# One half unit of weights moved between two visits of the RWKV group loop

## The chip, the cores and the metric

The kernel runs on one core of one Trainium2 chip. The metric is the device time in microseconds (us). Before the change three runs took 3044.5, 3040.24 and 3040.24 us, so the median is 3040.24 us.

## The reference

A trunk of two layers on 256 tokens of width 2048. Layer 0 is a mixer whose first half is stick-breaking attention (8 heads of 128) and whose second half is an RWKV-7 group (16 heads of 64), layer 1 a gated delta rule; each is followed by a residual and norm and by a squared-ReLU MLP of width 8192. Everything is float32. The part that matters here is the RWKV group and the attention beside it:

```
z = q @ k.T * d**-0.5;  log_keep = where(mask, log_sigmoid(-z), 0)
a = exp(where(mask, z + reverse_cumsum(log_keep), -inf));  o_sb = a @ v
w_log = -softplus(-(w0 + tanh(w_lo) @ w_up)) - 0.5;  decay = exp(-exp(w_log))
a = sigmoid(a0 + a_lo @ a_up);  g = sigmoid(g_lo) @ g_up
kk = l2_normalize(k * k_k);  k = k * (1 + (a - 1) * k_a)
S = S * w_t - (S kk_t) (kk_t a_t)^T + v_t k_t^T;  y_t = S r_t      # per token, per head
y = (y - mean(y)) * rsqrt(var(y) + eps) * lnx_g + lnx_b            # per head
o_rw = (y + sum(r * k * r_k) * v) * g
h = concat(o_sb, o_rw) @ w_out
```

The kernel computes the recurrence in four chunks of 64 tokens: inside a chunk a triangular inverse by doubling (five levels), between chunks a state handed on.

## The kernel before, in words

**Weights.** Every matrix product takes its weights from HBM in units of 256 input rows (two halves of 128) by 384 or 512 columns; a panel has 8 units. The product is done as three: `wh x ah`, `wh x al`, `wl x ah`. So each unit goes through three engines before TensorE can use it. SP loads it into `raw` (8 buffers), ScalarE casts it to `wh` (L887), VectorE subtracts to get the low half `wl` (L1357); `wh` and `wl` have 4 buffers each. TensorE then does the unit in two halves of 9 matmuls of 256 columns (narrow, mode B) or 6 of 512 (wide, mode A), all recorded at L421. Semaphores: `landed`, `hi_ready`, `lo_ready` forward, `unit_used` back.

**Groups and visits.** Layer 0's input projection is one panel for the low-rank parts and eight groups of two narrow panels (16 units, 32 halves). While group i is projected, the mixer of group i-1 (`mix0`) is computed. The mixer is a generator on each of TensorE, ScalarE and VectorE with the same 28 stops, here called visits 0 to 27. At each visit an engine does its part of the mixer and then the weights that the table `HOPS0` gives to that visit. The order is thus written out by hand and each engine's queue is strictly in this order. `hop_of(half, halves, hops)` turns the table, read as shares, into the visit of each half. On TensorE `drive` does the halves of a visit one by one. On ScalarE and VectorE `interleave` does the cast or subtraction of unit u+2 (`LEAD` = 2) at the visit where TensorE does the first half of unit u, that is half 2u. With `wait` = 1 the projection's results are copied out of the accumulator one visit after the last half of a panel.

`HOPS0` is used by six rounds of a loop and by one written out after it (mixers 0 to 6). `HOPS0Z` is the same table with a last share of 4; with it the eighth mixer is interleaved with 28 wide units of the output projection, 56 halves over 35 shares.

**The visits that matter**, on TensorE (with the lines that feed them):

- 1: low-rank products (L498 to L501), the values turned and the scores (L504 to L507).
- 2: the norm of the keys, L512. 3: the running sum of the logs, L517 and L518.
- 4: the attention product, L521 and L522; it waits for the exp of ScalarE, L980, which waits for VectorE's L1535. In between, ScalarE makes gates and powers (L949 to L977; L971 reads L512's result), VectorE the scan and the operands (L1510 to L1539; L1535 reads L518's result).
- 5: the Gram products, L534. 6: the turned operands, L550; ScalarE copies them (L989, L991).
- 7 to 17: five doublings of the inverse. At an odd visit X is turned and multiplied (L557, L565), VectorE masks the product (L1565); at an even visit the update (L581), VectorE adds it (L1572). From the third doubling on VectorE also does a piece of the next group's token shift at each visit.
- 18: L604 and L610. 19 to 25: the four chunks. L634 gives what is added to the state, VectorE scales it (L1597 for chunk 0, L1599 for the others) and adds the old state (L1602); the next chunk's L622 or L625 reads the new state; L638 and L639 give the chunk's output. Chunk n's first matmul (L622, L625) is at visits 20, 22, 24, its output at 19, 21, 23, 25.
- 26: the norm's mean, L644, after ScalarE has copied the four outputs (L1026). 27: the variance, L648.

The PSUM banks, the semaphores and the arithmetic of all these are not touched by the change.

Of the kernel before, what the change touches and what calls it, by code (L numbers as in the profile page):

```python
# [56 lines left out]
B_MLP1 = B_OUT1B + 8  # L57


HOPS0 = (3, 3, 2, 2, 2) + 16 * (1,) + (0, 1, 0, 1, 0, 1, 1)  # L60
HOPS0Z = HOPS0[:-1] + (4,)
HOPS_LORA = 16 * (1,)
HOPS1S = (3, 3, 3, 3, 3, 2, 3) + 14 * (1,) + (3, 2, 3, 3, 3)
# [56 lines left out]
def interleave(mixer, hops, units, one, ends, hook, ahead, begun=False, late=None, u0=0,  # L120
               wait=None):

    if not begun:
        for u in range(LEAD):
            one(u0 + u)
    wait = wait or (1 if mixer else 2)
    hops = hops if mixer else units * (1,)
    for y in range(len(hops) + wait + 1):  # L130
        if mixer and y < len(hops):
            next(mixer)
        for u in range(units):
            if hop_of(2 * u, 2 * units, hops) == y and (ahead or u + LEAD < units):
                one(u0 + u + LEAD)
        for j, e in enumerate(ends):
            after = y - hop_of(2 * e + 1, 2 * units, hops) - wait
            if after in (0, 1):
                hook(j, after)
    if mixer:  # L140
        assert next(mixer, "over") == "over"
    if late:
        late()
# [20 lines left out]
def trunk(nc, stop, x, w384, w512, wba, consts, c0, c1, prm0, lora, conv, rows1, normw, ln, out):  # L164
    ctx = ExitStack()
    with ctx:
# [209 lines left out]
        def _(pe):  # L376
# [58 lines left out]
            def drive(one, units, u0=0, mixer=None, hops=()):  # L435

                if mixer is None:
                    for u in range(units):
                        one(u0 + u)
                    return  # L440
                for y in range(len(hops)):
                    next(mixer)
                    for h in range(2 * units):
                        if hop_of(h, 2 * units, hops) == y:
                            one(u0 + h // 2, h % 2)
                assert next(mixer, "over") == "over"
# [204 lines left out]
            def group0(i):  # L651
                return blocks(i * 2 + P_GROUPS0, i * 2 + P_GROUPS0, "B", A, (0, 1), NARROW)
# [4 lines left out]
            with pe.Fori(1, GROUPS - 1) as i:  # L657
                drive(group0(i), 2 * UNITS, 0, mix0(i - 1), HOPS0)
            drive(group0(GROUPS - 1), 2 * UNITS, 0, mix0(GROUPS - 2), HOPS0)

# [217 lines left out]
        def _(act):  # L878
# [164 lines left out]
            def group0(i, first=False, last=False):  # L1043
                n = i * 2 + P_GROUPS0

                def one(u):
                    if last and u >= 2 * UNITS:
                        split(P_OUT0, u - 2 * UNITS, WIDE)
                    else:
                        split(n + u // UNITS, u % UNITS, NARROW)  # L1050

                def hook(j, after):
                    if after:
                        return
                    used(n, j * UNITS + UNITS - 1)
                    if j == 0:
                        if not first:

                            act.wait_ge(S("shifted"), i * 2 - 1)
                        nc.scalar.copy(pb[:, :, 1:T + 1], r2(pp[0][:, 0:3 * T], a=3)).then_inc(S("evacuated"), 1)  # L1060
                    else:
                        if not first:

                            act.wait_ge(S("scores"), i)
                        st(go(sbq[:, 0, :], pp[1][:, 0:T], ACT.Copy, scale=SB_SCALE))
                        nc.scalar.copy(sbq[:, 1:3, :], r2(pp[1][:, T:3 * T], a=2)).then_inc(S("evacuated"), 1)
                return 2 * UNITS, one, (7, 15), hook, True, True

            def wide(n):
                return lambda u: split(n + u // UNITS, u % UNITS, WIDE)  # L1070
# [7 lines left out]
            with act.Fori(1, GROUPS - 1) as i:  # L1078
                st.enter(i - 1, PER)
                interleave(mix0(i - 1), HOPS0, *group0(i))  # L1080
            st.leave(GROUPS - 2)
            interleave(mix0(GROUPS - 2), HOPS0, *group0(GROUPS - 1, last=True))
            interleave(mix0(GROUPS - 1), HOPS0Z, 28, wide(P_OUT0), (), nothing, True, begun=True)
# [259 lines left out]
        def _(dve):  # L1343
# [281 lines left out]
            def narrow(n, last=False):  # L1625
                def one(u):
                    if last and u >= 2 * UNITS:
                        split(P_OUT0, u - 2 * UNITS, WIDE)
                    else:
                        split(n + u // UNITS, u % UNITS, NARROW)  # L1630
                return one
# [15 lines left out]
            with dve.Fori(1, GROUPS - 1) as i:  # L1647
                st.enter(i - 1, PER)
                interleave(mix0(i - 1), HOPS0, 2 * UNITS, narrow(i * 2 + P_GROUPS0), (), nothing, True, True)
            st.leave(GROUPS - 2)  # L1650
# [429 lines left out]
```

## Time and profile before

| | |
|---|---|
| median of 3 runs | 3040.24 us |
| profiled execution | 3040.92 us |
| its span | 3039.3 us |
| TensorE busy | 2956.7 us |
| VectorE busy | 1797.6 us |
| ScalarE busy | 1452.7 us |
| read from HBM | 486.76 MB |

The profile is of one execution. Busy times overlap, so they don't add up to the span. A matmul's start is recorded and its end is modelled, so consecutive matmuls overlap in the timeline, and "idle before" is measured from a modelled end. Times in the timeline count from the span's start. The first mixer round begins at about 71 us, the eighth ends at about 580 us.

### The profile page before, as it was taken

The page shows a single profiled execution, that of the slowest core. Times are in us where ns is not written, and L with a number is a line of the kernel's source. Part 1 is how long each engine was busy: PE and PEld are TensorE (multiplying, and loading weights), DVE is VectorE, ACT ScalarE, POOL GpSimd, SP SyncE. Part 2 cuts the span into 40 slices and gives each one's busy share as a digit, 9 for nine tenths or more (in the row PEclk, how much of TensorE's full clock was granted, in tenths as well). Part 3 has the DMA queues.
Part 4 walks back from the last instruction along what each step waited for, and adds up shares of the span by engine and source line. Part 5 has one row for each costly group of instructions (what it writes and reads, how often), then busy time and mean ns, then how long its engine had stood idle before and what let it go on. Part 6 is the DMA issues. An engine that isn't in the chain of part 4 may idle for free.

```text
span 3039.3 us, 55921 instructions
## 1 busy us (share of the span) xinstructions
PE 2956.7 (97%) x22084; PEld 2603.5 (86%) x22084; DVE 1797.6 (59%) x2375; ACT 1452.7 (48%) x2241; POOL 13.1 (0%) x28
## 2 busy tenths in 40 slices
PE   8999999899999999999999999999999999999997
PEld 8888887688888888889999997999977888888886
DVE  4655565665554555564667665566667545555565
ACT  4544544344443434435566664556654434444442
POOL 0000000000000000000000000000000000000000
PEclk9999999999999999999999999999999999999998
DMA  7333334455555555544333433544335555555553
GB/s 231 109 111 106 107 118 139 166 202 193 189 189 191 186 194 188 192 160 139 120 139 133 139 133 136 177 141 137 133 122 219 189 192 187 194 191 191 193 188 111
DMA packets 156999, 491.86 MB, mean 162 GB/s; under 512 B 15584, under 2 KB 50528, under 8 KB 155776
## 3 DMA queue, kind: packets, MB, share of 16 engines
q1 hardware_dynamic: 154032, 476.18, 45.9%
q0 software_dynamic: 2224, 11.69, 1.0%
q8 instruction: 160, 2.62, 0.3%
q10 hardware_dynamic: 544, 1.05, 0.1%
q14 instruction: 39, 0.32, 0.0%
HBM read 486.76 MB, written 2.10 MB: 161 GB/s over the span
## 4 chain that ended last, share of the span: by engine, by line
PE 91%; DVE 5%; ACT 2%; issue 1%; DMA 0%; ACTq 0%; SPq 0%; DVEq 0%
PE pp L421 45%; PE mp L421 11%; PE pp L405 8%; PE mp L405 8%; PE pp L407 4%; PE mp L407 4%; PE mp L820 1%; PE mp L784 1%; PE mp L768 1%; PE mp L760 1%; DVE wl L1357 1%; ACT wh L887 1%; PE mp L826 1%; PE mp L565 0%; PE mp L581 0%
## 5 line engine op out<-in xcount | busy, mean ns | idle before, releaser
L1357 DVE TENSOR_TENSOR wl<-raw,wh 128x1024 fp32r<-128x1024 f32 (+1 forms) x936 | 1101.2, 1184 | 842.5 <-ACT wh L887 839.5
L887 ACT CAST wh<-raw 128x1024 fp32r<-128x1024 f32 (+1 forms) x936 | 944.1, 1018 | 856.4 <-PE pp L421 284.9
L421 PE MATMUL pp<-aT,wh 128*128 128x256 f32 x4704 | 897.6, 291 | 4.8 <-DVE wl L1357 4.8
L421 PEld LDWEIGHTS pp<-aT,wh 128*128 128x128 f32 x4704 | 733.0, 191 | 20.4 <-issue 5.5
L421 PE MATMUL pp<-aT,wl 128*128 128x256 f32 x2352 | 665.7, 283 | 0.0
L421 PEld LDWEIGHTS pp<-aT,wl 128*128 128x128 f32 x2352 | 450.0, 191 | 0.0
L405 PE MATMUL pp<-aT,wh 128*128 128x512 f32 x1024 | 364.0, 400 | 0.1
L421 PE MATMUL pp<-wh,hTh 128*128 128x512 f32 x896 | 358.6, 400 | 4.0 <-DVE wl L1357 2.6
L405 PE MATMUL mp<-aT,wh 128*128 128x512 f32 x1024 | 360.0, 396 | 0.0
L421 PE MATMUL pp<-wh,hTl 128*128 128x512 f32 x896 | 349.7, 390 | 0.0
L421 PE MATMUL pp<-wl,hTh 128*128 128x512 f32 x896 | 349.2, 390 | 0.0
L407 PE MATMUL pp<-aT,wl 128*128 128x256 f32 x1024 | 287.9, 281 | 0.0
L407 PE MATMUL mp<-aT,wl 128*128 128x256 f32 x1024 | 286.5, 280 | 0.0
L405 PEld LDWEIGHTS pp<-aT,wh 128*128 128x128 f32 x1024 | 194.0, 189 | 47.4 <-issue 0.7
L405 PEld LDWEIGHTS mp<-aT,wh 128*128 128x128 f32 x1024 | 192.2, 188 | 46.3
L421 PEld LDWEIGHTS pp<-wh,hTh 128*128 128x128 f32 x896 | 168.2, 188 | 42.1 <-DVE wl L1357 2.9
L421 PE MATMUL mp<-wh,hTl 128*128 128x512 f32 x512 | 199.2, 389 | 0.0
L421 PE MATMUL mp<-wh,hTh 128*128 128x512 f32 x512 | 199.2, 389 | 0.0
L421 PE MATMUL mp<-wl,hTh 128*128 128x512 f32 x512 | 199.2, 389 | 0.0
L421 PEld LDWEIGHTS pp<-wh,hTl 128*128 128x128 f32 x896 | 168.2, 188 | 35.9
L421 PEld LDWEIGHTS pp<-wl,hTh 128*128 128x128 f32 x896 | 168.4, 188 | 32.9 <-issue 0.5
L407 PEld LDWEIGHTS pp<-aT,wl 128*128 128x128 f32 x1024 | 194.8, 190 | 0.1
(301 smaller groups left out, 2673.5 us busy)
## 6 DMA issues: line engine op xcount, KB each, us to landing
raw<-in_w_dram SPq DMA_DIRECT2D x800, 512.0 KB, 3.3
raw<-in_w_dram SPq DMA_DIRECT2D x136, 384.0 KB, 3.5
ws<-in_ln_dram POOLq DMA_DIRECT2D x8, 1024.0 KB, 7.5
out_dram<-xres SPq DMA_DIRECT2D x8, 256.0 KB, 2.1
ws<-in_lora_dram POOLq DMA_DIRECT2D x8, 192.0 KB, 3.5
xres<-in_x_dram ACTq DMA_DIRECT2D x2, 512.0 KB, 6.4
xres<-in_x_dram SPq DMA_DIRECT2D x2, 512.0 KB, 7.2
ws<-in_c_dram POOLq DMA_DIRECT2D x1, 576.0 KB, 7.0
```

Source lines behind the costliest of these rows:

```text
L405: mm(o, wh[:, slot, kk, c], aT[:, k, :, :].rearrange("p a b -> p (a b)"), start=first is not None and kk == 0, stop=False, skip_group_chec ...
L407: last = mm(o[:, 0:T], wl[:, slot, kk, c], ah[:, k, :], start=False, stop=end and kk == 1, skip_group_check=True)
L421: last = mm(o, lhs, rhs, start=opens and m == 0, stop=end and kk == 1 and m == 2, skip_group_check=True)
L760: last = nc.tensor.transpose(mb[2][:, h * P:(h + 1) * P], Xc[:, 2 * h:2 * h + 2, :].rearrange("p c t -> p (c t)"), ident)
L768: last = mm(mb[hf][half(c), h * P:h * P + 32], At[half(hf), c, h, half(hf)], Xp[:, :, 0, :], start=h == 0, stop=True, skip_group_check=True)
L784: last = mm(mb[2 + c][half(hf), h * P:h * P + 32], XTc[half(c), h, hf, :], Yn1[half(c), 4 * hf + h, :], start=h == 0, stop=True, skip_grou ...
L820: last = mm(bank[:, h * P:(h + 1) * P], lhs[:, h, :], rhs[:, h, :], start=h == 0, stop=True, skip_group_check=True)
L826: last = mm(bank[:, j * T:(j + 1) * T], lhs[:, j, :], rhs[:, 2 * j:2 * j + 2, :], start=j == 0, stop=True, skip_group_check=True)
L887: nc.scalar.copy(wh[:, q % RING, :, 0:width], raw[:, q, :, 0:width]).then_inc(S("hi_ready"), 1)
L1357: tt(wl[:, q % RING, :, 0:width], raw[:, q, :, 0:width], f(wh[:, q % RING, :, 0:width]), ALU.subtract).then_inc(S("lo_ready"), 1)
```

## The change

One share is taken from visit 1 and one is given to visit 25. `HOPS0Z` is built from `HOPS0` and changes with it.

```diff
-HOPS0 = (3, 3, 2, 2, 2) + 16 * (1,) + (0, 1, 0, 1, 0, 1, 1)
+HOPS0 = (3, 2, 2, 2, 2) + 16 * (1,) + (0, 1, 0, 1, 1, 1, 1)
 HOPS0Z = HOPS0[:-1] + (4,)
```

Worked out with `hop_of`, the halves of a round of 32 fall like this (number of the half at each visit):

```
visit   0      1      2    3    4      5   6  ... 20  21  22  23  24  25  26  27
before  0 1 2  3 4 5  6 7  8 9  10 11  12  13 ... 27  -   28  -   29  -   30  31
after   0 1 2  3 4    5 6  7 8  9 10   11  12 ... 26  -   27  -   28  29  30  31
```

The casts and subtractions (even halves) are at visits 0, 0, 1, 2, 3, 4 both times, and then at 5, 7, 9, 11, 13, 15, 17, 19, 22, 26 before and at 6, 8, 10, 12, 14, 16, 18, 20, 24, 26 after. The copy out of the first panel (ScalarE, L1060) goes from visit 9 to visit 10.

## Rows read from the trace of the kernel before

**Rows 1.** The page, busy time of TensorE: us, share, instructions.

```profile
...
PE 2956.7 (97%) x22084; PEld 2603.5 (86%) x22084; DVE 1797.6 (59%) x2375; ACT 1452.7 (48%) x2241; POOL 13.1 (0%) x28
...
```

**Rows 2.** Waits of TensorE, 0 to 700 us: total, times, longest, all us.

```profile
...
PE mp L521 <- ACT ws L980: 8.1, 7, 1.2
...
PE mp L644 <- ACT ws L1026: 6.9, 8, 0.9
PE mp L471 <- DVE xres L1441: 6.9, 4, 5.3
PE pp L421 <- DVE wl L1357: 5.1, 11, 1.4
PE mp L625 <- DVE ws L1602: 3.9, 7, 0.9
...
```

**Rows 3.** Timeline of TensorE, attention product: start, length, instruction, idle before.

```profile
...
74.32 0.48 PE L421 MATMUL pp<-aT,wh 128*128 128x256 f32 x2
...
77.63 0.59 PE L512 MATMUL mp<-ws 128*128 128x256 f32 x2
...
80.86 0.39 PE L518 MATMUL mp<-ws,cc 128*128 128x128 f32 x2
81.00 0.48 PE L421 MATMUL pp<-aT,wh 128*128 128x256 f32 x2
...
84.55 0.70 PE L521 MATMUL mp<-ws 128*128 128x256 f32 x2 [1.16 <-ACT ws L980]
85.09 0.39 PE L522 MATMUL mp<-ws 128*128 128x128 f32 x2
85.72 0.50 PE L421 MATMUL pp<-aT,wh 128*128 128x256 f32 x2 [0.25 <-DVE wl L1357]
...
```

**Rows 4.** Timeline of TensorE, last chunk to the norm's mean.

```profile
...
121.21 0.50 PE L421 MATMUL pp<-aT,wh 128*128 128x256 f32 x2
...
122.39 0.55 PE L638 MATMUL mp<-ws 128*128 128x64 f32 x4
122.78 0.44 PE L639 MATMUL mp<-ws 128*128 128x128 f32 x2
124.07 0.70 PE L644 MATMUL mp<-ws 128*128 128x256 f32 x2 [0.85 <-ACT ws L1026]
...
```

**Rows 5.** Timeline of ScalarE, the exp before the attention product.

```profile
...
83.97 0.53 ACT L980 ACTIVATE ws<-ws 128x384 f32<-128x384 f32 x1 [0.90 <-DVE ws L1535]
...
```

**Rows 6.** Waits of ScalarE and VectorE for TensorE, 60 to 600 us.

```profile
...
ACT ws L971 <- PE mp L512: 0.4, 1, 0.4
...
DVE ws L1535 <- PE mp L518: 2.3, 1, 2.3
...
```

**Rows 7.** Timelines of ScalarE, VectorE and TensorE, first doubling.

```profile
...
92.51 0.37 ACT L991 COPY ws<-mp 128x256 f32<-128x256 f32 x1
...
93.80 0.84 ACT L887 CAST wh<-raw 128x768 fp32r<-128x768 f32 x1
...
94.67 0.96 DVE L1357 TENSOR_TENSOR wl<-raw,wh 128x768 fp32r<-128x768 f32 x1 [1.19 <-ACT wh L887]
95.54 0.28 DVE L1572 TENSOR_TENSOR ws<-ws,mp 128x128 f32<-128x128 f32 x1
...
94.48 0.43 PE L581 MATMUL mp<-ws 64*64 64x32 f32 x16
...
```

**Rows 8.** Timelines of VectorE and TensorE, third and last chunk.

```profile
...
119.03 0.96 DVE L1357 TENSOR_TENSOR wl<-raw,wh 128x768 fp32r<-128x768 f32 x1 [0.32 <-ACT wh L887]
120.03 0.35 DVE L1599 SCALAR_TENSOR_TENSOR ws<-mp,ws 128x128 f32<-128x128 f32 x1
...
119.30 0.38 PE L634 MATMUL mp<-ws 128*128 128x128 f32 x2
...
```

**Rows 9.** Windows: length, busy per engine, granted clock, DMA share, GB/s.

```profile
...
84.00:124.00 40.00, 37.73 (x492) 34.04 (x492) 23.14 (x49) 16.44 (x32) 0.00 (x0) 1.00 0.38 120
...
606.00:612.00 6.00, 4.11 (x16) 2.91 (x17) 5.89 (x10) 1.75 (x3) 0.00 (x0) 0.50 0.00 0
...
```

## The prediction

> **What bounds the kernel now.** I read the page first: TensorE is busy for 97% of the span [rows 1], so a change can pay only where TensorE waits, and costs what it makes TensorE wait. Next the waits of TensorE over the first 700 us, where the RWKV visits lie [rows 2]. The reader is to see that they are few: 8.1 us before the attention product (L521), 6.9 us before the norm's mean (L644), 5.1 us for low halves of weights (L421), 3.9 us for the last chunk's state (L625). Then the timeline of TensorE over one loop round. It repeats: L521 starts at 84.55 us [rows 3] and every 59.53 us after that, with the same waits to 0.01 us, so one round can be worked out. There are eight mixer rounds: six in the loop, a seventh written out with the same table, an eighth in which the output projection fills the visits (56 halves by 35 shares).
>
> The printed idle time is taken against a modelled matmul end, so I count from start to start. From L518 (80.86) to the next matmul without a wait are 0.14 us; so L522 (85.09) would be followed at 85.23, but the next half starts at 85.72 [rows 3]: 0.49 us lost where 0.25 are printed. From L639 (122.78, so the next could start at about 122.93) to L644 (124.07) are 1.14 us, where 0.85 are printed [rows 4].
>
> One half unit is 9 matmuls. Alone between two steps it takes 1.18 us (121.21 to 122.39) [rows 4]; three in a row take 3.31 us (74.32 to 77.63) [rows 3], so one more or less in a run is (3.31 - 1.18) / 2 = 1.07, with the 9 matmuls at 0.12 us 1.08 us.
>
> **The change, part by part.** Nothing is added or taken away on any queue: the same 32 halves, casts, subtractions and DMAs. Old half 5 leaves visit 1; from there each half is done one place later (visits 2 to 24 hold the half before the one they held), and visit 25 gets half 29. The cast on ScalarE and the subtraction on VectorE hang on the even halves, so between visits 5 and 20 they change from odd visits to even ones, and one goes from visit 22 to 24. SP's next load of a unit follows its subtraction by up to two visits; no engine waits for a landing in these rounds, so 0.
>
> *Visits 1 to 3, ahead of the attention product.* TensorE comes 1.08 us earlier to L512, L517 and L521. What L521 waits for is the exp L980 (83.97), which waits for a subtraction of VectorE, L1535 [rows 5]. Does this chain wait for TensorE anywhere between the scores and L521? In the eight rounds ScalarE waited for the key norm (L971) once, 0.4 us, and VectorE for the running sum (L1535) once, 2.3 us [rows 6], both in the eighth. In the other seven the chain is bound by its own engines, and the casts and subtractions of visits 0 to 4 are the same in number and place. So L521 stays at 84.55 and the wait before it grows by the whole 1.08 us, from 1.16 to about 2.24 printed: 0. If the chain did follow TensorE it would be a gain of 1.08; that end is a rival.
>
> *Visit 4.* Before, the first half there is the first of unit 5, whose low part comes late (0.25 printed, 0.49 from start to start) [rows 3]. After, the second half of unit 4 stands there, whose weights lie ready, and unit 5 comes 1.08 us later. The loss goes: -0.49 a round. Next late would be the operands of L534; on VectorE they stand ahead of the very subtraction that ended at 85.7, so they are there.
>
> *Visit 6 and the first doubling (a new wait).* VectorE now has a subtraction at visit 6, ahead of the masked product L1565 of visit 7. It needs the cast, which ScalarE can begin only behind the copy L991 (92.51, 0.37 long): about 92.78 to 93.62 with the 0.84 of the cast at 93.80. The subtraction runs until about 94.61, L1565 starts near 94.52 (0.87 behind it, as 94.67 to 95.54) and ends near 94.81; L581, now at 94.48 [rows 7], would start near 94.87. That is +0.39 a round. From below 0 (the cast gets ahead of the copy), from above a whole subtraction, 0.96; I take the worked one. At the other doublings the subtraction stands behind the state sum (0.28) and a shift piece (0.48), 1.8 us ahead of the next masked product: 0.28 + 0.48 + 0.96 fit, no wait.
>
> *Visits 18 to 24.* Before, the subtraction of visit 22 (119.03, 0.96 long) holds back L1599, which starts at 120.03 although L634 (119.30, 0.38 long) was done at 119.7 [rows 8]. It moves to visit 24, where VectorE idles: -0.24 at L625. The new ones at visits 18 and 20 come ahead of L1597 and L1599. By the same hand count L1597 comes 0.45 us later against a reserve of 0.7 at the next L622, and L1599 0.07 later, without reserve. Net -0.17. The floor here is -0.50 (all of L625's printed wait), the ceiling +0.96 (a subtraction wholly in the way).
>
> *Visit 25.* Half 29 takes 1.15 to 1.2 us where 1.14 are lost; what L644 waits for is ready 1.27 us after L639's start, and 0.15 + 1.15 of these are now used. The wait disappears and L644 keeps its distance to L639 within 0.05: 0. The end of the round (halves 30 and 31, the next round's visit 0, the norm's chain to the next scores) hangs on L644 and moves with it.
>
> Sum of a steady round: 0 - 0.49 + 0.39 - 0.17 + 0 = -0.27 us; seven rounds -1.9. The cover that visit 1 gave up is paid in full (1.08), and that won at visit 25 is worth as much (1.14 less the half itself): they cancel, and what is left are side effects.
>
> *Round seven* has at visit 22 a wide subtraction (1.2 us), so a wait of 0.9 at L625 (the longest) [rows 2] shrinks by 0.4 more. *Round eight:* visits 1 to 4 hold 3, 4, 3, 3 halves in place of 5, 3, 3, 4. Its wait is one of 1.4 us at L421 (the longest) [rows 2], before the first half of unit 7, behind VectorE's 2.3 us for L518 [rows 6]. After, L518 comes one half of this kind (1.37 us, 6 matmuls of 0.23) earlier and the wait moves to unit 6, 2.9 us long; L521 stays with one half less done, 1.38, of which visit 25 gives back 1.14: +0.25. All rounds: -1.9 - 0.4 + 0.25 = about -2.05 us.
>
> The profiled execution took 3040.92 us around a span of 3039.3; the sum puts it at 3038.9. The median of the runs shown is 3040.24, 0.68 lower, so the forecast is 3038.2 us.
>
> By printed idle times the sum would be 1.08 - 0.85 - 0.25 + 0.39 - 0.17 = +0.2 a round, +1.4 in all. The Trainium skill, Perfetto Trace Analysis (Tensor Engine Instruction), has a matmul's reported end as an estimate; the 0.25 us by which the row at 80.86 outlasts the next start agrees, so I stay with starts.
>
> **The rivals.**
> - *The chain to L521 follows TensorE.* For it: one wait each at L971 and L1535; against it: both in round eight. It gives 1.08 more in each of seven rounds: 3038.2 - 7.6 = 3030.6 us.
> - *No new wait at the first doubling*: 0.39 x 7 less, 3035.5 us. For it there is only that the order isn't seen in any row of before.
> - *The subtractions on even visits cost more.* A late L1597 (visit 19) crosses the 0.25 us left before L622, or L581 starts slowly after its wait. From there each round loses what is over; at 0.6 (two thirds of a subtraction) the time is 3038.2 + 4.2 = 3042.4 us, slower than before, though within the bound.
> - *The clock falls.* TensorE idles 2.24 us at L521 instead of 1.16. In 84 to 124, which holds the waits of a whole round, it was granted 1.00 (2.4 GHz); after the idle of 5.3 us before L471 [rows 2] it was granted 0.50 (1.2 GHz) in 606 to 612, with 4.11 us busy [rows 9]. Some 6 us busy at half speed until it rose again are 3 us lost; seven times 21: 3059 us, slower by over the bound. It decides where a wait of 2.24 us is enough to bring the clock down; the waits at full clock in [rows 2] reach to 1.4 us. The Trainium skill, TensorE: Matmul & The Clock Gate (What's actually happening), has the throttled state as the default that activity lifts; the row at 0.50 agrees in kind.
>
> **How the numbers follow.** Forecast 0.72; no new wait 0.11; dearer even visits 0.09; chain follows TensorE 0.05; clock 0.03. A measurement of this kernel can tell about 0.2% (6.1 us) from no change; the first three cases lie within it but for 0.01 of the second and 0.01 of the third. Faster: 0.05 + 0.01 = 0.06; slower: 0.03 + 0.01 = 0.04; same 0.90. Range: from below the second case to above the third, 3033 to 3043 us; outside are the fourth and fifth and the tails. The runs of before were 3040.24 twice and 3044.5, so they scatter more than the change weighs.
>
> **What the profile after would show.** L521's wait near 2.24 us in the first seven rounds; none at L644, and none at L421 right behind L522; a new one of about 0.3 us at L581 of the first doubling; L625's down from 0.50 to about 0.25; a round of 59.26 us in place of 59.53; in round eight 2.9 us before a half of L421. I would be wrong if L521's wait didn't grow (the chain moved), if L644's stayed, or if a granted clock under 1.00 stood between 60 and 490 us.

## The result, and the profile after

The changed kernel takes 3049.22 us (median of 8 runs, 3048.27 to 3052.18) where the kernel before took 3040.89 beside it (8 runs, 3038.35 to 3044.5). The ratio is 1.0029 with a 95% interval of 1.0021 to 1.0038: 8.3 us slower by the medians. The forecast was 3038.2 us and a range up to 3043. The profiled execution took 3052.18 us, its span is 3050.5.

The page, busy time of TensorE, against [rows 1]:

```profile
...
PE 2967.1 (97%) x22084; PEld 2613.9 (86%) x22084; DVE 1796.1 (59%) x2375; ACT 1455.0 (48%) x2241; POOL 13.1 (0%) x28
...
```

TensorE does the same 22084 matmuls but is busy 10 us longer. Matmuls that take longer mean a lower clock, not a wait. Next the waits of TensorE over the first 700 us, against [rows 2] (total, times, longest, in us):

```profile
...
PE mp L521 <- ACT ws L980: 13.2, 7, 1.9
...
PE pp L421 <- DVE wl L1357: 4.7, 4, 2.7
PE mp L581 <- DVE ws L1565: 2.8, 7, 0.4
PE mp L622 <- DVE ws L1602: 2.4, 7, 0.4
PE mp L625 <- DVE ws L1602: 1.7, 7, 0.6
...
```

L644 is gone, L521 went from 8.1 to 13.2 us, L581 came in with 0.4 us a round, L625 fell to 0.2 in the loop, L622 rose. All of this was forecast in kind, and the forecast's sum of it is a gain of 2; it doesn't explain a loss of 8 us. So I looked at the granted clock. These are windows of 6 us from each L521 on, one for each of the seven rounds, and then one from the wait of 2.7 us for a low half (L421) in round eight (length, busy time of each engine, granted clock, DMA share, GB/s), against [rows 9]:

```profile
...
84.00:90.00 6.00, 5.28 (x50) 5.04 (x54) 3.88 (x8) 2.35 (x4) 0.00 (x0) 0.72 0.42 132
145.00:151.00 6.00, 5.57 (x80) 5.19 (x80) 4.97 (x10) 2.20 (x4) 0.00 (x0) 1.00 0.46 146
204.00:210.00 6.00, 5.34 (x51) 5.15 (x55) 3.91 (x8) 2.35 (x4) 0.00 (x0) 0.72 0.42 132
265.00:271.00 6.00, 5.61 (x70) 5.33 (x70) 3.55 (x7) 2.16 (x4) 0.00 (x0) 0.72 0.47 147
326.00:332.00 6.00, 5.90 (x82) 5.52 (x83) 4.96 (x10) 1.87 (x4) 0.00 (x0) 1.00 0.47 146
385.00:391.00 6.00, 5.68 (x70) 5.49 (x70) 3.48 (x7) 2.09 (x4) 0.00 (x0) 0.72 0.48 159
446.00:452.00 6.00, 5.94 (x71) 5.59 (x72) 3.51 (x7) 1.83 (x4) 0.00 (x0) 0.72 0.50 158
514.00:520.00 6.00, 5.33 (x16) 4.28 (x17) 3.93 (x4) 0.97 (x2) 0.00 (x0) 0.72 0.59 195
...
```

The clock was granted in full behind L521 in rounds two and five only. In rounds one, three, four, six and seven, and in round eight behind its own wait, the mean is 0.72: read in steps of 1 us, 1.00 (2.4 GHz) at first, then 0.50 (1.2 GHz) for some 3 us. Such a stretch is called a fall below. In the same windows of the kernel before every round reads 1.00. In all 8 runs of the changed kernel the mean clock is 0.988 or 0.989, in the profiled run of before 0.992.

What a fall costs is read by comparing rounds. TensorE in round two, which has none, against [rows 3] and [rows 4]; first from L512 to L534:

```profile
...
137.31 0.28 PE L421 MATMUL pp<-aT,wl 128*128 128x256 f32 x1
137.69 0.70 PE L512 MATMUL mp<-ws 128*128 128x256 f32 x2
...
145.43 0.70 PE L521 MATMUL mp<-ws 128*128 128x256 f32 x2 [1.88 <-ACT ws L980]
...
146.11 0.48 PE L421 MATMUL pp<-aT,wh 128*128 128x256 f32 x2
146.43 0.28 PE L421 MATMUL pp<-aT,wl 128*128 128x256 f32 x1
...
148.43 0.78 PE L534 MATMUL mp<-ws 64*64 64x128 f32 x20
...
```

And in round one, which has one:

```profile
...
84.72 0.70 PE L521 MATMUL mp<-ws 128*128 128x256 f32 x2 [1.89 <-ACT ws L980]
85.26 0.39 PE L522 MATMUL mp<-ws 128*128 128x128 f32 x2
85.40 0.52 PE L421 MATMUL pp<-aT,wh 128*128 128x256 f32 x2
85.72 0.41 PE L421 MATMUL pp<-aT,wl 128*128 128x256 f32 x1
85.94 0.63 PE L421 MATMUL pp<-aT,wh 128*128 128x256 f32 x2
86.36 0.41 PE L421 MATMUL pp<-aT,wl 128*128 128x256 f32 x1
...
89.23 1.10 PE L534 MATMUL mp<-ws 64*64 64x128 f32 x32
...
```

The two halves of visit 4 take 2.32 us in round two (146.11 to 148.43) and 3.83 us in round one (85.40 to 89.23); a group of three matmuls there takes 0.64 us (85.94 to 86.58) where it takes 0.36. From L521 to the next L521 are 59.23 us behind rounds two and five (145.43 to 204.66) and 60.71 to 60.74 behind rounds one, three, four and six. So a fall costs 1.5 us. Without one the round is 0.30 us shorter than the 59.53 of before: the forecast was 0.27.

The books of the two profiled executions: from L521 of round one to that of round seven +4.15 us, which is four falls of 1.49 less six times 0.30; from there to L644 of round eight +3.04 us (136.14 for 133.10), which holds the falls of rounds seven and eight. Together +7.2 us, in a difference of medians of 8.3. The profiled span is longer by a further 4 us, behind the RWKV rounds; single runs of either kernel differ by as much, so they aren't taken apart here. But one more fall lies there, in layer 1, behind a wait that the change doesn't touch. It is the wait for a low half of weights; first the changed kernel, then the kernel before, each with the window of 6 us behind it:

```profile
...
1429.81 0.51 PE L421 MATMUL pp<-aT,wh 128*128 128x256 f32 x2 [1.75 <-DVE wl L1357]
...
1430.00:1436.00 6.00, 6.00 (x39) 6.00 (x39) 6.00 (x12) 5.55 (x10) 0.00 (x0) 0.72 0.54 182
...
```

```profile
...
1423.28 0.50 PE L421 MATMUL pp<-aT,wh 128*128 128x256 f32 x2 [1.76 <-DVE wl L1357]
...
1423.00:1429.00 6.00, 5.52 (x44) 5.32 (x45) 6.00 (x12) 5.26 (x9) 0.00 (x0) 1.00 0.48 161
...
```

The same wait of 1.76 us is followed by a fall in one kernel and by none in the other.

### The profile page after: what moved, and what is told of

The parts are those of the page before. It is cut to its first block, busy times and chain, and to the rows that moved or that the text cites. A ratio compares the mean times of both kernels' runs of the same rounds, so it can differ in the third digit from the quotient of the medians.

```text
span 3050.5 us, 55919 instructions
## 1 busy us (share of the span) xinstructions
PE 2967.1 (97%) x22084; PEld 2613.9 (86%) x22084; DVE 1796.1 (59%) x2375; ACT 1455.0 (48%) x2241; POOL 13.1 (0%) x28
## 4 chain that ended last, share of the span: by engine, by line
PE 91%; DVE 5%; ACT 3%; issue 2%; DMA 0%; ACTq 0%; SPq 0%; DVEq 0%
PE pp L421 45%; PE mp L421 11%; PE pp L405 8%; PE mp L405 8%; PE pp L407 4%; PE mp L407 4%; PE mp L820 1%; ACT wh L887 1%; PE mp L784 1%; PE mp L768 1%; PE mp L760 1%; DVE wl L1357 1%; PE mp L826 1%; PE mp L581 0%; DVE xres L1437 0%
## 5 line engine op out<-in xcount | busy, mean ns | idle before, releaser
L421 PE MATMUL pp<-aT,wh 128*128 128x256 f32 x4704 | 906.9, 293 | 2.8 <-DVE wl L1357 2.8
L421 PEld LDWEIGHTS pp<-aT,wh 128*128 128x128 f32 x4704 | 740.5, 193 | 16.9 <-issue 5.5
L421 PE MATMUL pp<-aT,wl 128*128 128x256 f32 x2352 | 670.1, 285 | 0.0
L421 PEld LDWEIGHTS pp<-aT,wl 128*128 128x128 f32 x2352 | 454.5, 193 | 0.0
L421 PE MATMUL pp<-wh,hTh 128*128 128x512 f32 x896 | 359.1, 401 | 5.4 <-DVE wl L1357 4.0
L421 PE MATMUL pp<-wh,hTl 128*128 128x512 f32 x896 | 350.4, 391 | 0.0
L421 PE MATMUL pp<-wl,hTh 128*128 128x512 f32 x896 | 349.7, 390 | 0.0
L421 PEld LDWEIGHTS pp<-wh,hTh 128*128 128x128 f32 x896 | 168.7, 188 | 43.5 <-issue 3.6
L421 PEld LDWEIGHTS pp<-wh,hTl 128*128 128x128 f32 x896 | 168.5, 188 | 36.0
L421 PE MATMUL mp<-wh,hTh 128*128 128x512 f32 x512 | 199.2, 389 | 0.0
L421 PE MATMUL mp<-wl,hTh 128*128 128x512 f32 x512 | 199.2, 389 | 0.0
L421 PE MATMUL mp<-wh,hTl 128*128 128x512 f32 x512 | 199.2, 389 | 0.0
L421 PEld LDWEIGHTS pp<-wl,hTh 128*128 128x128 f32 x896 | 168.8, 188 | 33.0 <-issue 0.5
```

Of the source, the lines that this page charges most:

```text
L421: last = mm(o, lhs, rhs, start=opens and m == 0, stop=end and kk == 1 and m == 2, skip_group_check=True)
```

## The experiments

Theory A: the wait before L521, 1.16 us before and 1.9 after, is now long enough that TensorE's clock falls. Theory B: the slowdown comes from what moved on the other engines (subtractions at even visits) or from the half at visit 25. Falls in the table are counted over the seven rounds of one profiled execution, by the granted clock behind L521. Those in round eight and in layer 1 come on top and are gathered behind experiment 10. Ratios are to the kernel before on the same chip.

| kernel | wait at L521, us | falls | round without, with a fall, us | ratio, 95% interval |
|---|---|---|---|---|
| before | 1.16 | 0 | 59.53 | |
| changed | 1.89 | 5 | 59.23, 60.72 | 1.0029 (1.0021 to 1.0038) |
| 1: visit 1 to 4 | 1.9 | 6 | 60.07, 61.57 | 1.0057 (1.0043 to 1.0071) |
| 2: visit 4 to 25 | 1.16 | 0 | 58.67 | 0.9972 (0.9963 to 0.9981) |
| 3: changed, filled | 0.59 | 0 | 59.21 | 1.0005 (0.9996 to 1.0014) |
| 4: changed, filled less | 1.45 | 0 | 59.21 | 0.9997 (0.9988 to 1.0006) |
| 5: two from visit 1 | 1.15 and 1.17 | 0 | 60.08 | 1.0005 (0.9995 to 1.0014) |
| 6: visit 20 to 25 | 1.16 | 0 | 58.79 | 0.9982 (0.9973 to 0.9991) |
| 7: changed, two tables | 1.89 | 4 | 59.0, 60.5 | 1.0000 (0.9991 to 1.0009) |
| 8: as 2, two tables | 1.16 | 0 | 58.44 | 0.9970 (0.9958 to 0.9982) |
| 9: changed, filled least | 1.71 | 1 | 59.23, 60.71 | 1.0003 (0.9993 to 1.0014) |
| 10: changed, late exp | 2.97 | 7 | -, 61.8 (63.1 in round one) | 1.0059 (1.0042 to 1.0075) |

**1. The longer wait alone.**

```diff
-HOPS0 = (3, 3, 2, 2, 2) + 16 * (1,) + (0, 1, 0, 1, 0, 1, 1)
+HOPS0 = (3, 2, 2, 2, 3) + 16 * (1,) + (0, 1, 0, 1, 0, 1, 1)
```

> Built from the kernel before; one half goes from visit 1 to visit 4, nothing else moves: visit 25 stays empty, the casts and subtractions from visit 5 on stay at the odd visits. Theory A (the longer wait before L521 lets TensorE's clock fall to 1.2 GHz): the wait printed is 1.9 us as in the changed kernel, the granted clock falls to 0.50 behind it in most of the seven rounds, and a round is 59.53 + 1.08 - 0.49 = 60.1 us without a fall and 61.6 with one; with five falls and one in round eight the time is 3040.9 + 4.1 + 9 = about 3054 us. Theory B (the slowdown comes from the subtractions at even visits and from the half at visit 25): neither is here, no fall matters, 3040.9 + 4.1 = about 3045 us.

3057.65 us against 3041.65. Behind L521 of rounds one, two and seven:

```profile
...
82.00:88.00 6.00, 5.33 (x79) 5.10 (x79) 3.89 (x9) 3.08 (x5) 0.00 (x0) 1.00 0.44 132
142.00:148.00 6.00, 5.26 (x30) 5.21 (x31) 3.90 (x8) 3.18 (x5) 0.00 (x0) 0.72 0.40 126
...
450.00:456.00 6.00, 5.45 (x31) 5.40 (x31) 3.79 (x7) 3.15 (x5) 0.00 (x0) 0.72 0.46 140
...
```

Rounds two to seven fall, round one doesn't. The tail and the even visits are as before, and yet the falls are there: A. The falls are six, as many as expected, but all in the seven rounds and none in round eight. The time is 3.7 us above the expected; one more fall in layer 1 is part of it, the rest stays open.

**2. The same tail, the half from visit 4.**

```diff
-HOPS0 = (3, 3, 2, 2, 2) + 16 * (1,) + (0, 1, 0, 1, 0, 1, 1)
+HOPS0 = (3, 3, 2, 2, 1) + 16 * (1,) + (0, 1, 0, 1, 1, 1, 1)
```

> Built from the kernel before; the half for visit 25 is taken from visit 4, behind the attention product, instead of visit 1; from visit 5 on the order is that of the changed kernel. Theory A (clock): the wait before L521 stays at 1.16 us, no fall; a round is 59.53 - 1.08 (visit 4) + 0.39 (L581) - 0.15 (L622 and L625) = 58.7 us, so seven rounds give -6 us: about 3035 us. Theory B (even visits and visit 25): it is as slow as the changed kernel, 3046 to 3049 us.

3031.93 us against 3041.65: faster than both kernels. Its waits of TensorE over 700 us show the old L521 and the new L581 side by side, and L644 doesn't appear:

```profile
...
PE mp L521 <- ACT ws L980: 8.2, 7, 1.2
...
PE mp L581 <- DVE ws L1565: 2.8, 7, 0.4
...
```

From visit 5 on this kernel is the changed one, so B is refuted. The time is 3 us below the expected: round eight was left out of that sum, and it is 1.5 us shorter (70.71 us from round seven's L521 to its own, before 72.19).

**3 and 4. The wait filled with useless work.** Both are built on the changed kernel; the edit of 3, and in 4 a single matmul of 256 columns:

```diff
+                for _ in range(2):
+                    mm(mb[3][:, 0:384], tri, sbb, start=True, stop=True, skip_group_check=True)
                 pe.wait_ge(S("attn"), m1)
```

> Built from the changed kernel; two matmuls of 384 columns (1.3 us together) whose result is overwritten stand at visit 4 ahead of the wait for the exp. They do no useful work; they only keep TensorE busy in the time in which it would wait. Theory A (clock): the wait printed falls from 1.9 to about 0.6 us, L521 doesn't start later, no clock falls, every round is 59.23 us: 3040.9 - 2.1 = about 3039 us, that is 1.5 us less for each fall avoided. Theory B (order of the other engines): useless work can't help, 3049 us.

> As the kernel with two filling matmuls, but one of 256 columns (about 0.4 us): the wait printed is about 1.5 us, between the 1.16 of before and the 1.9 of the changed kernel. Theory A: fewer falls than the five of the changed kernel, each still worth 1.5 us; 3039 to 3046 us. Theory B: 3049 us. If the falls are as many as with 1.9 us, the length of the wait between 1.5 and 1.9 doesn't decide.

3043.03 and 3041.61 us against 3041.65. The timeline of TensorE in 3, round two (the fill moved the lines: L523 is the attention product), and the windows of 4 behind the attention product of rounds one and seven:

```profile
...
143.22 0.70 PE L523 MATMUL mp<-ws 128*128 128x256 f32 x2 [0.59 <-ACT ws L982]
...
```

```profile
...
82.00:88.00 6.00, 5.36 (x79) 5.11 (x79) 4.97 (x10) 2.35 (x4) 0.00 (x0) 1.00 0.41 132
...
437.00:443.00 6.00, 5.07 (x76) 4.82 (x77) 4.98 (x10) 2.35 (x4) 0.00 (x0) 1.00 0.38 118
...
```

No round of either falls. Adding some 10 or 3 us of useless matmuls takes away 7 to 9 us against the changed kernel, each taken against the kernel before beside it: the strongest sign for A, for nothing else was moved. In round eight, where the fill doesn't stand before the wait of 2.7 us, 3 still has a fall and 4 has none. There the attention product doesn't wait either, so the fill of 3 costs its own 1.3 us (512.25 to 513.54); with the fall it is the larger part of the 4 us by which 3 stays above its expected 3039.

**5. Two halves taken from visit 1** (on the changed kernel).

```diff
-HOPS0 = (3, 2, 2, 2, 2) + 16 * (1,) + (0, 1, 0, 1, 1, 1, 1)
+HOPS0 = (3, 1, 2, 2, 3) + 16 * (1,) + (0, 1, 0, 1, 1, 1, 1)
```

> Built from the changed kernel; one more half goes from visit 1 to visit 4, so that two fewer stand ahead of L521 than before. Theory A (how long TensorE idles before L521, with where in time it falls, decides whether the clock falls): part of the added idleness shows at L512, the rest at L521, at least 2.2 us in all there; the clock falls in all seven rounds instead of five or six, each costing 1.5 us, and a fall-free round would be 59.23 + 0.6 to 1.08 = about 60 us: 3041 + 7 x 0.7 + 7 x 1.5 + 2 = about 3058 us. Rival (a fall happens with a fixed share of rounds whatever the wait): again five or six of seven, about 3056 us; the granted clock of each round tells them apart, not the time.

3042.67 us against 3040.99, and no fall: a miss. It wasn't a longer wait, as I had meant it, but two short ones:

```profile
...
PE mp L512 <- ACT ws L955: 8.2, 7, 1.2
PE mp L521 <- ACT ws L980: 8.1, 7, 1.2
...
```

TensorE idles more than in the changed kernel (2.3 us a round in these two places), but in pieces of 1.2 us with 6 us of matmuls between them, and the clock stays. Half 4 went to visit 2, and with it one of the two casts that ScalarE did between L955 and L980 went behind L980. So L521 comes 7.01 us behind L512 (76.62 to 83.63), not 7.74; that is why the second wait didn't grow.

**6. The half from visit 20** (on the kernel before).

```diff
-HOPS0 = (3, 3, 2, 2, 2) + 16 * (1,) + (0, 1, 0, 1, 0, 1, 1)
+HOPS0 = (3, 3, 2, 2, 2) + 15 * (1,) + (0,) + (0, 1, 0, 1, 1, 1, 1)
```

> Built from the kernel before; the half for visit 25 is taken from visit 20, between two state chunks; through visit 19 nothing changes, so casts and subtractions stay at odd visits. Theory A: L521's wait stays 1.16 us, no fall; L644's wait goes (-1.14 + half), at visit 20 TensorE waits about 0.5 us for U instead of doing the half of 1.15: a round is 0.5 to 0.8 us shorter, 3041.6 - 4 to 5.5 = about 3037 us. Theory B (a half at visit 25 itself does harm): no faster than before, 3042 us or more.

3034.91 us against 3040.99, rounds of 58.79 us. A half moved from visit 20 to visit 25 is a gain; one at visit 25 does no harm.

**7 and 8. Two tables.** TensorE's `drive` gets a table of its own, ScalarE and VectorE keep `HOPS0`. In 7 it is the changed table, in 8 that of 2:

```diff
+HOPS0P = (3, 3, 2, 2, 1) + 16 * (1,) + (0, 1, 0, 1, 1, 1, 1)
-                drive(group0(i), 2 * UNITS, 0, mix0(i - 1), HOPS0)
+                drive(group0(i), 2 * UNITS, 0, mix0(i - 1), HOPS0P)
```

> TensorE follows the changed table, ScalarE and VectorE keep the table of before: TensorE's halves move as in the changed kernel, the casts and subtractions don't. Theory A (clock): the wait before L521 is still 1.9 us and the clock still falls in five or six of seven rounds; only the 0.39 us at L581 and the 0.35 at L622 change: 3049 - 2 = about 3047 us. Theory B (the subtractions at even visits): the slowdown is gone, 3039 us or less.

> The half for visit 25 from visit 4 on TensorE alone; ScalarE and VectorE keep the table of before. Against the kernel with the half from visit 4 on all engines (round 58.67 us, 0.39 of it the wait at L581): the L581 wait goes, the waits at L622 and L625 are 0.19 and 0.50 as before instead of 0.35 and 0.19: a round of about 58.4 us, no fall: 3031.9 - 2 = about 3030 us. Rival (the wait moves on to the next product of the doubling): 3032 us, the same.

7 takes 3041.09 us against 3040.99: 6 us less than expected, though the falls haven't gone. Behind the attention product of rounds one and two:

```profile
...
84.00:90.00 6.00, 5.59 (x66) 5.39 (x70) 3.61 (x7) 3.02 (x5) 0.00 (x0) 0.72 0.46 134
144.00:150.00 6.00, 5.06 (x76) 4.81 (x77) 4.98 (x10) 3.08 (x5) 0.00 (x0) 1.00 0.36 116
...
```

Rounds one, three, five and six fall (60.5 us), two, four and seven don't (59.0); round eight has none, for its wait of 2.7 us has gone too, and from L523 of round seven to that of round eight are 68.90 us where the kernel before has 72.19. So the useful part of the change and four falls cancel here. By time alone this would have spoken for B; the clock of each round speaks for A. That a round with the same wait of 1.9 falls or not, and that round eight stopped waiting so long, I hadn't counted on. 8 takes 3032.45 us against 3040.99; the L581 wait is gone and the rounds are 58.44 us, 0.23 less than in 2. The medians don't resolve this: by time alone it could as well be the rival, "3032 us, the same"; it is the length of the rounds that speaks against it.

**9. A still shorter fill** (one matmul of 64 columns) and **10. A later exp** (both on the changed kernel). The edit of 10 (`PER` is the number of ScalarE's counted steps in a round; the two copies add two):

```diff
                 act.wait_ge(S("loga"), m1)
+                for _ in range(2):
+                    st(nc.scalar.copy(sba, sba))
+                    st.settle()
                 go(sba, sba, ACT.Exp).then_inc(S("attn"), 1)
-            PER = 16
+            PER = 18
```

> As the kernel with one filling matmul, but of 64 columns: the wait printed before L521 is about 1.7 us, between the 1.45 us at which no clock fell in seven rounds and the 1.9 at which it fell in four to six. Theory (the length of one unbroken wait decides, with its place in time): some rounds fall, fewer than with 1.9, zero to four; time 3041 to 3047 us.

> Built from the changed kernel; ScalarE copies a tile onto itself twice between its wait for VectorE and the exp L980, which makes L521 later by 0.9 to 1.1 us in one unbroken wait of 2.8 to 3.0 us. The copies change no value. Theory (the length of one unbroken wait decides): the clock falls in all seven rounds, where the wait of 1.9 gave five; a round without a fall would be 59.23 + 1.0, with it 61.7 us; 3039 + 7 + 10.5 + 2 = about 3058 us. Rival (a fixed share of the rounds falls, whatever the wait over 1.5 us): five or fewer falls again, about 3055 us; the granted clock of each round tells it.

9: 3042.61 us against 3041.43; a wait of 1.71 us and one fall, in round one, with round two after it free:

```profile
...
84.00:90.00 6.00, 5.32 (x50) 5.13 (x54) 3.94 (x8) 2.35 (x4) 0.00 (x0) 0.72 0.40 128
145.00:151.00 6.00, 5.60 (x80) 5.21 (x81) 4.97 (x10) 2.18 (x4) 0.00 (x0) 1.00 0.48 147
...
```

10: 3058.98 us against 3041.43; a wait of 2.97 us and a fall in every round, in rounds one and seven one of double length:

```profile
...
85.00:91.00 6.00, 5.77 (x30) 5.37 (x34) 2.61 (x4) 2.01 (x4) 0.00 (x0) 0.50 0.50 140
148.00:154.00 6.00, 5.71 (x70) 5.38 (x70) 2.67 (x5) 2.07 (x4) 0.00 (x0) 0.72 0.50 145
210.00:216.00 6.00, 5.94 (x71) 5.68 (x72) 2.62 (x5) 1.83 (x4) 0.00 (x0) 0.72 0.57 157
271.00:277.00 6.00, 5.13 (x42) 4.88 (x46) 3.25 (x5) 2.61 (x5) 0.00 (x0) 0.72 0.45 133
333.00:339.00 6.00, 5.29 (x47) 4.98 (x50) 3.09 (x4) 2.45 (x5) 0.00 (x0) 0.72 0.46 130
395.00:401.00 6.00, 5.41 (x62) 5.10 (x66) 2.97 (x4) 2.35 (x4) 0.00 (x0) 0.72 0.44 132
457.00:463.00 6.00, 5.71 (x30) 5.31 (x34) 2.66 (x4) 2.06 (x4) 0.00 (x0) 0.50 0.51 143
...
```

Over the kernels the falls rise with the one unbroken wait: none of seven at 0.59, 1.16 and 1.45 us, one at 1.71, four to six at 1.9, seven at 2.97. One fixed share for all waits over 1.5 us doesn't fit one of seven at 1.71 beside seven of seven at 2.97. Each count is that of one profiled execution.

The falls outside the seven rounds say the same, and something more. Behind the wait of 2.74 us in round eight the clock fell in four kernels (changed, 3, 9, 10) and didn't in two (1, 4). Behind the wait of 1.75 or 1.76 us in layer 1, which stands in all twelve kernels and which no edit touches, it fell in seven (changed, 1, 2, 4, 5, 7, 9) and didn't in five (before, 3, 6, 8, 10). So the length of the wait makes a fall more likely and doesn't decide it alone.

## Why the prediction was wrong

*The step that failed* is the choice between the forecast and the fourth rival, "the clock falls". In the forecast's sum the clock is put at nothing; the runs show six falls, 9 us, in its place. The rival named the place (L521), the cause (a wait grown by what visit 1 gave up) and the sign; I gave it 0.03, because the waits of before at full clock reached 1.4 us in [rows 2] and the one behind which it had fallen was 5.3, and took the gap between as if it were on my side. Nothing in the rows said so, and the trace of before holds a narrower gap that I didn't read. At 1423.28 it has the wait of 1.76 us at full clock. And the wait of 5.3 us at L471 begins at about 601.0 and ends at 606.29, while the clock falls well inside it:

```profile
...
603.00:604.00 1.00, 0.00 (x0) 0.00 (x0) 1.00 (x2) 0.00 (x0) 0.00 (x0) 0.94 0.00 0
604.00:605.00 1.00, 0.00 (x0) 0.00 (x0) 0.86 (x4) 0.47 (x3) 0.00 (x0) 0.50 0.00 0
...
```

So some 2.8 us of idling had been enough there. The forecast wait of 2.24 us lay between these two, where the trace was silent; that bound should have been in the range.

*Its price was mis-sized*: 3 us for each of seven falls. A fall behind L521 measures 1.5 us, since the half clock lasts some 3 us there and not the 8 from L471's start on (606.29 to about 614.1), and there are five of seven and one in round eight. 6 x 1.5 = 9.0, less 7 x 0.30 = 2.1, gives +6.9 against 7.2 in the profiled rounds. The 0.3 are in rounds seven and eight: without their falls they come out level (+3.04 less 2.98), where the forecast had some 0.4 us of gain.

*Right, by the same rows.* In round two: from L521 to L534 3.00 us (before 3.51): -0.51, forecast -0.49. L581 late behind the subtraction of visit 6:

```profile
...
154.01 0.96 DVE L1357 TENSOR_TENSOR wl<-raw,wh 128x768 fp32r<-128x768 f32 x1 [1.71 <-ACT wh L887]
154.89 0.28 DVE L1565 TENSOR_TENSOR ws<-mp,cc 128x128 f32<-128x128 f32 x1
...
155.32 0.43 PE L581 MATMUL mp<-ws 64*64 64x32 f32 x16 [0.39 <-DVE ws L1565]
...
```

The order is the one worked out: subtraction, L1565, then L581; from L534 to L581 6.89 us (before 6.42): +0.47, forecast +0.39. From L581 to L644 29.39 (before 29.59): -0.20, forecast -0.17. L639 and L644 of round one, without a wait:

```profile
...
124.15 0.44 PE L639 MATMUL mp<-ws 128*128 128x128 f32 x2
...
125.50 0.64 PE L644 MATMUL mp<-ws 128*128 128x256 f32 x2
...
```

1.35 us for a half and the step, where [rows 4] had 1.29 with nothing between. And L644 to the next L521 19.95 (before 20.00). Experiments 3 and 4 have just this kernel without the falls in seven rounds: their rounds are 59.21 us, the 0.3 us shorter that the forecast had, and in the whole time no difference from before can be measured.

*A size a little off.* L521's wait is 1.89 us, not 2.24: 0.26 us of the missing cover show at L512 (137.69, with the last matmul before it at 137.31 and 0.12 the usual step), which TensorE now reaches before ScalarE's square L955 is done. I had counted waits of before, where L512 had none, and not the slack it had.

*The chain of L521 doesn't follow TensorE* (third rival): confirmed, L512 to L521 grew from 6.91 to 7.74 us. That it can be shortened from the other side, by a cast moved out of it, came out in experiment 5.

*Left open*: why at 1.9 us one round falls and the next doesn't. Rounds of equal length and equal waits differ only in when the wait comes, so I think it is where in time the wait lies. The untouched wait in layer 1 is a sign of it: its length and the work around it stay the same, the edits only make it come earlier or later, and it is followed by a fall in seven of twelve kernels. What it is about the time that decides isn't shown; no run moved the start of a round with all else kept.

## What to carry to other kernels

A wait of the matmul engine that grows can have two prices: the time itself, and a lower clock once it is long and unbroken (here from 1.7 us on); the second isn't in the waits view and is found in the granted clock by window. Read it over the whole trace: an edit that only shifts later work in time can bring or take away a fall there. Take work from where it covers no long wait (visit 4 or 20 here: some 9 and 6 us faster) and leave it ahead of a wait. If a long wait can't be shortened, useless matmuls in front of it can be worth more than they cost (here they only won back the loss), or it can be split in two.

## What the runs showed of the hardware

- The clock fell to 0.50 behind a single wait of 1.9 us of an engine busy for 97% of the span, in 5 of 7 rounds of the changed kernel, and behind 1.71 us in 1 of 7; it didn't behind two of 1.2 us in the same round. Behind one and the same wait of 1.75 or 1.76 us in layer 1 it fell in 7 of 12 kernels.
- The low clock isn't tied to the wait's end: in round one of the changed kernel L521 starts at 84.72 and the first slow matmuls at about 85.7, when TensorE has been busy again for 1 us; over its five falls it is 0.5 to 1.5 us. In experiment 10 it begins inside the wait of 2.97 us in rounds one, six and seven. TensorE: Matmul & The Clock Gate of the Trainium skill (HAM oscillation) has this pattern of a pause in each round of a loop and a cold start behind it; its example pauses for 3 to 5 us, and the runs here show that 1.9 us is enough in most rounds.
